# Eight projections of a hybrid decoder layer: 576 token columns taken as 288 and 288 in place of 512 and 64

## The reference: one decoder layer for a prompt and a sample group

```
a_glu, b_glu, q, k, v, qi, ki, wi, g_c, g_a = split(h @ w_in)      # 512 each for a, b, q, k, v; 1024 each for g_c, g_a
glu  = a_glu * sigmoid(b_glu)
c    = silu(layer_norm(depthwise_conv31(concat(prefix, glu))))
conv_branch = c @ w_conv_out
scores = sum_h wi[h] * relu(qi[h] . ki)       # top 128 (prompt) or top 256 of 4104 keys (sample)
o    = softmax attention over the selected keys
attn_branch = o @ w_attn_out
mix  = (sigmoid(g_c + bias) * conv_branch + sigmoid(g_a + bias) * attn_branch) @ w_o
x1   = LN1(alpha * h + mix);   y = LN2(alpha * x1 + moe(x1) + sigmoid(x1 @ w_pg) * (p @ w_pp))
```

## Time and profile before

| | us |
|---|---|
| median of three runs | 1575.75 (1574.61 to 1577.5) |
| profiled execution, whole time | 1578.52 |
| its span | 1576.6 |
| PE busy | 1336.2 (85%) |
| DVE busy | 717.8 (46%) |
| POOL busy | 554.7 (35%) |
| ACT busy | 450.8 (29%) |

### The profile page before, as it was taken

How to read it: one execution, slowest core, us unless ns; L and a number is a source line. 1 busy time by engine, 2 the same in 40 slices (tenths; PEclk the granted TensorE clock), 3 DMA queues, 4 the chain that set the end, 5 groups by cost and what they waited for, 6 DMA issues and landing times.

```text
span 1576.6 us, 19143 instructions
## 1 busy us (share of the span) xinstructions
PE 1336.2 (85%) x7392; PEld 776.9 (49%) x7392; DVE 717.8 (46%) x1364; ACT 450.8 (29%) x928; POOL 554.7 (35%) x519
## 2 busy tenths in 40 slices
PE   5699998899577766678999999999997899999950
PEld 5524554575343333334554544887784444454420
DVE  2329999994574555534430013234351212222228
ACT  1540142641132333575453231113110111111110
POOL 1300196983653666542004541000003344444320
PEclk9899999899877877679999999899998999999985
DMA  7601211112643566533115654215607999999943
GB/s 245 223 1 56 73 63 54 54 63 84 181 134 112 161 173 176 145 112 89 54 43 154 212 168 141 87 39 178 236 7 294 421 380 418 375 407 419 410 184 100
DMA packets 87896, 272.95 MB, mean 173 GB/s; under 512 B 17303, under 2 KB 49767, under 8 KB 76855
## 3 DMA queue, kind: packets, MB, share of 16 engines
q1 hardware_dynamic: 49776, 157.25, 26.2%
q0 software_dynamic: 35552, 111.22, 22.5%
q10 hardware_dynamic: 2479, 3.27, 0.6%
HBM read 292.55 MB, written 22.98 MB: 200 GB/s over the span
## 4 chain that ended last, share of the span: by engine, by line
PE 56%; DVE 18%; DMA 10%; another core or an unknown queue 7%; ACT 5%; issue 3%; POOL 1%; ACTq 0%; SPq 0%; POOLq 0%; DVEq 0%
PE ps L1007 10%; PE ps L1326 7%; PE ps L1013 5%; PE ps L1184 5%; PE ps L1192 4%; PE ps L1350 4%; DVE arena L1716 4%; DVE arena L1715 4%; DVE arena L1717 4%; PE ps L1036 3%; DMA arena<-in_w_dn,arena 3%; PE ps L1071 2%; DMA arena<-scr_x,arena 2%; DMA arena<-in_w_pp 1%
## 5 line engine op out<-in xcount | busy, mean ns | idle before, releaser
L1007 PE MATMUL ps<-arena 128*128 128x64 f32 (+3 forms) x1216 | 345.1, 450 | 9.3 <-ACT arena L1521 8.7
L1007 PEld LDWEIGHTS ps<-arena 128*128 128x128 f32 (+1 forms) x1216 | 192.2, 203 | 157.7 <-issue 148.0
L907 POOL DMA_INDIRECT arena<-in_cache_k,arena x128 | 125.8, 983 | 261.9 <-PE ps L1036 189.8
L1326 PE MATMUL ps<-arena 128*64 128x256 f32 x1568 | 191.7, 387 | 6.6 <-DVE arena L2079 3.5
L917 POOL DMA_INDIRECT arena<-in_cache_v,arena x128 | 123.9, 968 | 84.1 <-PE ps L1074 49.4
L1326 PEld LDWEIGHTS ps<-arena 128*64 128x64 f32 x1568 | 109.6, 139 | 85.7 <-issue 29.6
L1036 PE MATMUL ps<-arena 128*128 128x128 f32 x512 | 88.7, 320 | 65.1 <-ACT arena L1428 42.8
L1396 ACT ACTIVATE arena<-ps 128x256 f32<-128x256 f32 (+5 forms) x148 | 60.7, 418 | 271.9 <-PE ps L1192 61.7
L1013 PE MATMUL ps<-arena 128*128 128x256 f32 (+5 forms) x640 | 127.0, 360 | 3.0 <-ACT arena L1530 1.6
L956 POOL DMA_INDIRECT arena<-scr_x,arena x49 | 49.7, 1014 | 194.5 <-DVE arena L2073 179.9
L1013 PEld LDWEIGHTS ps<-arena 128*128 128x128 f32 (+1 forms) x640 | 104.7, 185 | 24.9 <-issue 4.9
(11 more groups left out here) (317 smaller groups left out, 1700.2 us busy)
## 6 DMA issues: line engine op xcount, KB each, us to landing
arena<-in_w_gu SPq DMA_DIRECT2D x32, 2048.0 KB
arena<-in_w_dn SPq DMA_DIRECT2D x32, 1024.0 KB
arena<-in_w_in SPq DMA_DIRECT2D x20, 1024.0 KB
arena<-in_w_o SPq DMA_DIRECT2D x4, 1024.0 KB, 5.3
arena<-in_w_pg SPq DMA_DIRECT2D x4, 1024.0 KB
arena<-scr_ypair SPq DMA_DIRECT2D x4, 1024.0 KB, 6.3
arena<-in_x_prompt SPq DMA_DIRECT2D x4, 512.0 KB, 11.7
scr_h<-arena SPq DMA_DIRECT2D x4, 512.0 KB, 4.7
```

What stands on the lines that cost most here:

```text
L907: pl.indirect_dma_start(kunit[:, 2 * j + t, :], None, I["cache_k"], bass.IndirectOffsetOnAxis(ap=offs[:, t, n:n + 1], axis=0)).then_inc(k_ ...
L1007: mm = nc.tensor.matmul(out, w[:, k], hT[:, k, a:b], start=(k == 0), stop=(k == KC - 1))
L1326: mm = nc.tensor.matmul(PS[2 + p % 2][64 * half:64 * half + 64, 0:2 * P], xT[:, p % 3, j, 64 * h:64 * h + 64], w[:, k, half, :], start=(k ...
```

## The change

Seven of the eight kinds of projection with tokens as columns (b, a, k, q, gc, ga and cb) take columns 0 to 287 in the P job and 288 to 575 in the S job, so the S job now holds 224 prompt tokens and all 64 sample tokens. `ab` and `qiP` keep 512 (and 64). The evacuations follow; that of `aS` becomes two ACT instructions, because prompt and sample rows go to two places. The estimated costs follow too: 6.9 and 1.8 become 3.9 and 3.9; for cb 3.5 and 0.9 become 1.95 and 1.95 (DVE: 0.75 and 0.25 become 0.45 and 0.45). As these numbers decide order, jobs and products move.

```diff
+HN = N // 2
 ...
-    wide = {"bP": 6.9, "bS": 1.8, "aP": 6.9, "aS": 1.8, ... "gcP": 6.9, "gcS": 1.8, "gaP": 6.9, "gaS": 1.8, "cbP": 3.5, "cbS": 0.9, ...
+    wide = {"bP": 3.9, "bS": 3.9, "aP": 3.9, "aS": 3.9, ... "gcP": 3.9, "gcS": 3.9, "gaP": 3.9, "gaS": 3.9, "cbP": 1.95, "cbS": 1.95, ...
+def columns(kind):
+    if kind in ("abP", "abS"):
+        return (0, NP) if kind == "abP" else (NP, NS)
+    return (0, HN) if kind[2] == "P" else (HN, HN)
 ...
-                    mm = feature_rows(ps[:, :], weights(a[1] * P, a[1] * P + P), 0, NP)
+                    mm = feature_rows(ps[:, 0:HN], weights(a[1] * P, a[1] * P + P), 0, HN)
                 elif kind in ("gcS", "gaS"):
-                    mm = feature_rows(ps[:, 0:NS], weights(a[1] * P, a[1] * P + P), NP, N)
+                    mm = feature_rows(ps[:, 0:HN], weights(a[1] * P, a[1] * P + P), HN, N)
 ...
                     if kind == "aS":
-                        ins = nc.scalar.activation(gluS[:, c, :, PRE:], ps[:, 0:NS].rearrange("p (b q) -> p b q", b=NB), cp)
+                        nc.scalar.activation(gluP[:, c, PRE + HN:], ps[:, 0:NP - HN], cp)
+                        ins = nc.scalar.activation(gluS[:, c, :, PRE:], ps[:, NP - HN:HN].rearrange("p (b q) -> p b q", b=NB), cp)
```

More of the change, by code:

```diff
@@ L139, in cost @@
     kind, a = job[0], job[1:]
-    wide = {"bP": 6.9, "bS": 1.8, "aP": 6.9, "aS": 1.8, "kP": 6.9, "kS": 1.8, "qP": 6.9, "qS": 1.8, "ktok": 1.1, "v": 3.5, "gcP": 6.9, "gcS": 1.8, "gaP": 6.9, "gaS": 1.8, "cbP": 3.5, "cbS": 0.9, "abP": 3.5, "T": 0.9, "QK": 3.4, "EX": 0.0,
+    wide = {"bP": 3.9, "bS": 3.9, "aP": 3.9, "aS": 3.9, "kP": 3.9, "kS": 3.9, "qP": 3.9, "qS": 3.9, "ktok": 1.1, "v": 3.5, "gcP": 3.9, "gcS": 3.9, "gaP": 3.9, "gaS": 3.9, "cbP": 1.95, "cbS": 1.95, "abP": 3.5, "T": 0.9, "QK": 3.4, "EX": 0.0,
             "PT": 0.5, "PV": 2.7, "OS": 0.9, "cv": 0.5, "croot": 0.0, "cn": 0.5, "ncS": 0.5, "ncP": 0.5}
@@ L194, in vector_cost @@
         return 0.5 * (a[0] // H + 1) + 0.5
-    return {"gcP": 16.0, "cv": 1.5, "croot": 0.9, "cn": 0.7, "cbP": 0.75, "cbS": 0.25, "abP": 1.45, "QK": 1.0, "PT": 0.2, "PV": 0.8}.get(kind, 0.0)
+    return {"gcP": 16.0, "cv": 1.5, "croot": 0.9, "cn": 0.7, "cbP": 0.45, "cbS": 0.45, "abP": 1.45, "QK": 1.0, "PT": 0.2, "PV": 0.8}.get(kind, 0.0)
 def interleaved():
@@ L1176, in _ @@
                         pe.wait_ge(drained, after("oT"))
-                    at, n = (0, NP) if kind[2] == "P" else (NP, NS)
+                    at, n = columns(kind)
                     if kind[0] == "c":
@@ L1508, in _ @@
                     if kind == "aP":
[L1509 removed]
+                        ins = nc.scalar.activation(gluP[:, c, PRE:PRE + HN], ps[:, 0:HN], cp)
                     elif kind == "bP":
[L1511 removed]
+                        ins = nc.scalar.activation(convo[:, c, 0:HN], ps[:, 0:HN], ACT.Sigmoid)
                     else:
[L1513 removed]
+                        ins = nc.scalar.activation((kT if kind == "kP" else qT)[:, c, 0:HN], ps[:, 0:HN], cp)
                 elif kind in ("kS", "qS", "bS", "aS"):
@@ L1576, in _ @@
                         ins = nc.scalar.activation(csig[:, a[0] % 2, c, 0:rows], v, ACT.Sigmoid, scale=cvec[:, c, 32:33], bias=cvec[:, c, 33:34])
[L1577 to L1580, removed]
+                elif kind in ("cbP", "cbS", "abP", "abS"):
+                    ins = hand_over(job, columns(kind)[1])
                 elif kind in ("wo", "pp"):
@@ L1849, in gated_add @@
             def gated_add(kind, g, c):
-                at, n = (0, NP) if kind == "abP" else (NP, NS)
+                at, n = columns(kind)
                 m, ga = mixT[:, 2 * g + c, at:at + n], gaT[:, 2 * g + c, at:at + n]
@@ L1887, in _ @@
                 elif kind in ("cbP", "cbS"):
-                    at, n = (0, NP) if kind == "cbP" else (NP, NS)
+                    at, n = columns(kind)
                     m = mixT[:, 2 * a[0] + a[1], at:at + n]
```

18 lines of the change are left out of this document (10 added, 8 removed).

## The result

| | before | changed |
|---|---|---|
| median, us | 1576.62 (1574.61 to 1580.25) | 1554.32 (1549.14 to 1557.64) |
| profiled execution | 1578.52 | 1552.44 |
| its span | 1576.6 | 1550.6 |

The ratio is 0.9862, with a 95% interval of 0.9829 to 0.9895: 22 us less. The profiled executions stand 26.1 apart. The forecast was 1541, its range 1526 to 1564.

What follows compares the result with a forecast made beforehand. PE was taken as the bound up to `offs` and from 718 to 929, gathers between. Savings 24.5 + 3.1 + 2.9 + 6.2 + 1 less 1.5 gave 36: 1542.5 profiled, 1541 median, range 1526 to 1564.

Steps and rivals of the forecast that it cites:

- The price of a pair: PE's projection jobs: a P and S pair with 288 columns each takes 7.89 us, 0.77 less than 8.66.
- The rule that I had weighed: PE's weight loads: every load would be paid in both kernels, so a pair would save nothing; the prediction rejected it.
- Up to `offs`: Stretch up to `offs`: moved product stands and saved PE work bring `offs` to 379.6 from 391.9, 12.3 us.
- The gather stage: From `offs` to the first cb job: lead grows to 29 us at `PV(3)`, 24 or 25 kept at cb.
- the same seven are left, plus `QK(10)` and waits for it (3 to 5): cb starts at 694: Behind `PV(8)` at 640: seven attention units remain as before, so cb starts at 694 in place of 718.8.
- cb: The cb jobs between attention units: eight pairs save 0.39 us each, 3.1 in all.
- The ga stage: Four ga groups save two pairs of 0.77 us each, 6.2, less 1.5 for small stands; 27.5 a group.
- PE really stands at `QK(g)`: Rival, gather bursts: PE waits until the burst ends, ga groups 4.0 us longer, 12 slower overall, 1588; chance 0.06.
- the prediction's own sign: Ga stage: the forecast counts as wrong if the groups take over 29 us.
- the first rival: Whole kernel: only columns count, order leads come to nothing, 15.5 us saved where PE is the bound, 1562; chance 0.18.

Runs made afterwards that it cites:

- e3: The changed kernel with only the places of the convolution products put back to those of the kernel before: 1564.65 us, ratio 0.9944 to before.
- e1: The changed kernel's new columns only, with estimated costs, order and product places of the kernel before: 1555.27 us, ratio 0.9881 to before.
- e4: The changed kernel with the old order behind `offs` put back on all engines, new columns and product places kept: 1548.72 us, ratio 0.9840 to before.
- e5: The splice: the changed kernel with its order kept up to `T(6,3)`, the old order from there: 1533.13 us, ratio 0.9767 to before.
- e6: As e4, but three ga jobs ahead of `QK(11)` to `QK(13)` and DVE's taps dealt by new costs: 1532.80 us, ratio 0.9764 to before.
- e8: As e4, but the gaP job ahead of `QK(11)` to `QK(13)` does each matmul as two of 144 columns: 1535.80 us, ratio 0.9797 to before.
- e10: The changed kernel run once more, in the fourth comparison: 1482.22 us, ratio 0.9910 to before.
- e11: e4 run once more, in the fourth comparison: 1470.18 us, ratio 0.9807 to before.
- e12: e5 run once more, in the fourth comparison: 1481.18 us, ratio 0.9890 to before.
- e7: As e5, but with three ga jobs ahead of `QK` in three groups of the ga stage: 1533.57 us, ratio 0.9762 to before.

## Why the prediction was right and where it was wrong

**The price of a pair** was right: 7.77 against 7.89. Weight loads are covered in the new jobs: the trace has a load of 0.19 us for each matmul record, and these follow each other every 0.24 us. The rule that I had weighed, from the Trainium skill ("TensorE: Matmul & The Clock Gate", section The mechanism), that a load overlaps running matmuls only when the row group differs, does not hold here: all loads use all rows, and its forecast was no saving on a pair. (The same section also lets a load run ahead when it goes to the background weight buffer; no row here tells which buffer a load uses.)

**Up to `offs`** was right in size and reason: 378.67 against 379.6, of which 0.9 is this execution's early start, and e3 put the 10.4 us back by the product places alone.

**The gather stage** is where it failed. The sample groups came as forecast (`PV(0)` 428.9 against 430, `PV(2)` 477.6 against 480, `PV(3)` 508.4 against 512, first `pi` on DVE 493.6 against 494). The step that failed is "the same seven are left, plus `QK(10)` and waits for it (3 to 5): cb starts at 694". The seven are right, but it counted from `PV(8)`, as if the sample groups set when cb may start; `PV(8)` was 6 later than forecast (645.99 against 640), and the rest took 60.6 where 54 were counted. What sets cb is the prompt's chain, from its first `pi` on DVE through the selection rounds and attention units to the first cb job. Its start, DVE, in the kernel before and the changed one:

```profile
507.56 0.35 DVE L1805 TENSOR_SCALAR arena<-arena 128x256 f32<-128x256 f32 x1 [6.23 <-ACT arena L1396]
```

```profile
493.58 0.35 DVE L1814 TENSOR_SCALAR arena<-arena 128x256 f32<-128x256 f32 x1 [3.74 <-issue]
```

| kernel | `offs` | first `pi` on DVE | first cb job | `pi` to cb | `PV(5)` |
|---|---|---|---|---|---|
| before | 391.9 | 507.6 | 718.8 | 211.3 | 589.2 |
| changed | 378.7 | 493.6 | 706.6 | 213.0 | 558.2 |
| e1 | 388.7 | 495.7 | 709.0 | 213.3 | 578.6 |
| e3 | 389.1 | 503.2 | 715.0 | 211.8 | 568.0 |
| e4 | 379.5 | 488.2 | 699.0 | 210.8 | 571.1 |
| e5 (3rd comparison) | 380.3 | 493.0 | 687.5 | 194.5 | 557.6 |
| e6 (3rd) | 380.4 | 476.9 | 684.9 | 207.9 | 558.0 |
| e8 (3rd) | 377.4 | 480.3 | 688.0 | 207.6 | 560.9 |
| e10 (4th) | 378.4 | 481.0 | 646.7 | 165.8 | 530.6 |
| e11 (4th) | 380.1 | 460.1 | 633.1 | 173.0 | 521.6 |
| e12 (4th) | 379.5 | 482.3 | 642.2 | 159.9 | 531.9 |

In the first five rows `pi` to cb is 211 to 213 us whatever the order, while `PV(5)` moves by 31. So there a group done early is worth nothing to the first cb job; only an earlier `pi` is. In the later comparisons the stretch differs by some us between the new and the old order too. (The splice has the shortest: it begins `pi` one sample group later than the old order and has that group less behind it. That this is the reason is not shown.)

How late `pi` comes behind `offs` depends on the order. With the new columns and the new order it is 114.9 in the changed kernel and 114.1 in e3, against 107.0 and 108.7 with the old order (e1, e4). It is 112.7 in e5, where the splice still has the new order, against 96.5 and 102.9 (e6, e8), and 102.6 and 102.8 against 80.0 in the fourth comparison. The kernel before has 115.7, with its long gcP jobs. These are single executions, and e4 and e8, the same program up to there, differ by 6; but with the new columns the new order is later in every comparison.

Two chains lead to `pi` on DVE. In DVE's own list it stands behind all 62 taps of the convolution. On PE the new order has it behind `OS(2)`, the old one ahead of `EX(2)`; from PE it goes through ACT, which first issues nine output DMAs and then empties the bank. The changed kernel: PE's first `pi`, DVE's last taps, two rows of ACT (1626 is eight of the DMAs, 1406 the evacuation):

```profile
489.12 1.48 PE L1140 MATMUL ps<-arena 64*128 64x256 f32 x8
```

```profile
483.00 6.84 DVE L1801 SCALAR_TENSOR_TENSOR arena<-arena 128x512 f32<-128x512 f32 x14
```

```profile
490.27 2.74 ACTq L1626 DMA_DIRECT2D out_conv_s<-arena  x8
493.06 2.91 ACT L1406 ACTIVATE arena<-ps 128x256 f32<-128x256 f32 x8 [3.21 <-issue]
```

The same in e4: PE's first `pi`, DVE's last taps and its first `pi`:

```profile
475.89 0.70 PE L1153 MATMUL ps<-arena 64*128 64x256 f32 x2
```

```profile
474.03 7.83 DVE L1814 SCALAR_TENSOR_TENSOR arena<-arena 128x512 f32<-128x512 f32 x16
488.21 0.35 DVE L1827 TENSOR_SCALAR arena<-arena 128x256 f32<-128x256 f32 x1 [6.35 <-ACT arena L1419]
```

The last to come is ACT's evacuation, not the taps: DVE has stood idle for 3.74 us in the changed kernel, for 6.35 in e4 and for 6.23 before. (The profile names ACT in the last two; in the changed kernel it names none, but the evacuation began 0.5 us ahead.) PE comes to `pi` 13.2 us later in the changed kernel than in e4. e4 gains only 5.4 of these, as its ACT gets the last gc job only at 483.05, 1.3 us behind the end of a gather burst (481.77). About 3.2 us of the way are the output DMAs, in every kernel. The taps are late as well (their end is 489.84 against 481.86), since the last of them stand behind group 2 in DVE's list, so with `pi` early on PE they would be the next to hold it. How the taps are dealt out is not the cause by itself: e6 has the old order on PE with the taps dealt by the new costs, 26 tap records behind the maximum of group 2 where e4 and e8 have 16, and its `pi` follows the last tap at once, still earlier than in e8:

```profile
464.14 12.75 DVE L1859 SCALAR_TENSOR_TENSOR arena<-arena 128x512 f32<-128x512 f32 x26
476.93 0.35 DVE L1872 TENSOR_SCALAR arena<-arena 128x256 f32<-128x256 f32 x1
```

So what the record shows is that the order puts `pi` behind group 2, on PE and on DVE. A kernel with the new order but `pi` ahead of `EX(2)` was not run, nor one with the output DMAs moved away from `pi`.

The columns also gave more in this stage than their average. Before, a gcP job stood right ahead of `PV(0)` and a gcS and a gcP ahead of `PV(1)`. In e1 the first takes 4.92 in place of 8.24, the two others 9.33 in place of 11.85; the last S job, which grows, stands in a burst. From `offs` to `PV(3)` e1 takes 140.5 us against 149.1, 8.6 less, where four pairs are worth 3.1 by their price. I had named these pieces (8.24 and 11.85) but used them only for the order. This 5.5 more makes up for what the columns don't give in the ga stage.

**cb** was mis-sized, low. By the profile a pair costs 0.39 less, as forecast (jobs of 3.70 and 1.11 us become two of 2.21), 3.1 in all. Of the other 3, about 1.5 is the clock: before, the first two 512-column jobs took 5.33 and 5.12 at a granted clock of 0.68 and 0.72 of full speed, now only the first job is slow (3.80 at 0.57). The last 1.5 is idle time of PE in the stretch, 4.3 before and 2.9 now.

**The ga stage** failed as a term: 6.2 for pairs, less 1.5 for stands. PE's records come at full pace again 14.7 us behind the end of `PV` (839.35 to 854.05), and it gets 71 of them until the stand. Before, the gaP job ahead of `QK` filled 7 us with 16 records, 83 to 85 came through, and 0.4 to 0.7 was lost. With 288 columns 16 records last 3.9 us, `QK` comes sooner and stands. The prediction had this place as its tightest and computed that `PT` would not wait, which was right for groups 11 to 13 (0.40 at most) and not for group 14 (2.30, for ACT); it did not ask whether PE would be given its instructions. The rival "PE really stands at `QK(g)`" (0.06) had the place right, for another reason and at 2 us a group in place of 4. By the prediction's own sign, groups of over 29, this part is wrong. It also took all four groups to hold four ga jobs, and the third holds five. Where the stands are absent, in e10, two groups of four ga jobs take 27.0 each (748.1, 775.0, 802.1), against 27.5 forecast.

In all: the forecast won 36 from three things. Columns and product places gave 25 (e4, 24.8 in its comparison; e11, 26.3), about as much as their terms (12.3 for the product places and the gc pairs ahead of `offs`, 3.1, 3.1 and 6.2 for the other pairs); the order, from which it had counted a lead of 12 more at cb, cost 4 to 12 instead. So the sign of one third of the sum was wrong. The time, 13 us above the forecast, fell inside the range because columns and product places carried it and because the range had been drawn out to the first rival; that is in part luck.

Three slips in the working change nothing of this. 1542.5 less 2.8 is 1539.7, not 1541; 15.5 off the median of before gives the first rival 1560, not 1562; and the gather at 429.92 in the earlier trace rows is the last of its burst, not the last but one.

## What to carry to other kernels

A lead of one chain at some point is worth only what the chain that sets the next stage gains: before counting it, find that stage's first input, and follow what stands ahead of it in the in-order list of every engine that it passes. Cost tables that set an order also deal out the work of other engines: when an edit is meant to change sizes, run it with the old order too; here that beats the change itself, by 12 us in the fourth comparison. Where a stage has a phase in which an engine is given few instructions, put the ones with most time each into it; here three groups took 27.4 us each in place of 29.0 (e7, e5), though the whole time stayed within 1 us.

## What was not expected of the hardware

In the ga stage, while POOL issues a burst of gathers, PE gets 70 to 85 matmul records from the end of `PV` on, with about as many weight loads, and then mostly one to three each 0.7 us until 2 us behind the burst; e8 shows that the count matters. This holds for the traces of the first three comparisons. In the fourth the same kernels show no such stand.

The second point is where the 80 us between the comparisons come from. In the second comparison, DVE sees the result of `QK(4)` only when the burst is over. e4, PE's last part of `QK(4)`, and DVE's maximum of it:

```profile
530.40 2.34 PE L1074 MATMUL ps<-arena 128*8 128x320 f32 x32
```

```profile
540.50 0.49 DVE L1920 TENSOR_REDUCE arena<-ps 128x1 f32<-128x320 f32 x1 [9.11 <-remote]
```

In the fourth comparison, the same kernel as e11:

```profile
491.63 2.34 PE L1074 MATMUL ps<-arena 128*8 128x320 f32 x32
```

```profile
494.10 0.49 DVE L1920 TENSOR_REDUCE arena<-ps 128x1 f32<-128x320 f32 x1 [1.48 <-PE ps L1074]
```

There POOL issues at the same pace (0.94 and 0.30), yet DVE goes on 0.13 us behind PE and a group takes 16.6 us (484.0 to 500.6) in place of 25.2 (521.6 to 546.8). PE's stands in the ga stage are gone too. The span is 78 us shorter, and all of it lies between `offs` (379.5 and 380.1) and the transposes behind the last `PV` (953.4 and 875.4), where the gathers are. What differs between these executions isn't known; no run tells it. It isn't the chip alone, as the third and the fourth comparison ran on the same one. It means that a saving in this kernel has to be given with its own runs of the kernel before: the change is worth 22 us in the first comparison and 14 in the last.
